# One split instruction per weight granule in place of two, on two engines, in the expert loop of a two-layer trunk

## The reference

```
def swiglu(v, wg, wu, wd):
    return (jax.nn.silu(v @ wg) * (v @ wu)) @ wd

def moe_swiglu(v, router, wg, wu, wd):        # v: 256 x 1024
    ...                                       # combine: 256 x 8, two non-zero per token
    for e in range(N_EXPERTS):                # 8 experts, wg, wu: 1024 x 2816, wd: 2816 x 1024
        y = y + combine[..., e:e + 1] * swiglu(v, wg[e], wu[e], wd[e])
```

## Time and profile before

| | before |
|---|---|
| median of 3 runs | 1849.8 us (1849.54 to 1851.08) |
| profiled execution, own time | 1847.36 us |
| its span, first to last instruction | 1845.6 us |
| mean granted TensorE clock | 0.954 |
| PE busy | 1659.2 us, 90% of the span |
| DVE busy | 1309.2 us, 71% |
| ACT busy | 999.0 us, 54% |
| chain that ended last | PE 85%, DVE 7%, ACT 3% |

### The profile page before, as it was taken

One profiled execution on the slowest core, in us unless ns is written; L12 is line 12 of the kernel. 1 busy time (PEld: TensorE's weight loads), 2 busy tenths in 40 slices (PEclk: granted clock), 3 DMA queues, 4 the chain that ended last, 5 costly groups with the idle time before them and its releaser, 6 DMA issues.

```text
span 1845.6 us, 22715 instructions
## 1 busy us (share of the span) xinstructions
PE 1659.2 (90%) x7728; PEld 1355.5 (73%) x7728; DVE 1309.2 (71%) x1517; ACT 999.0 (54%) x1261; POOL 43.7 (2%) x73
## 2 busy tenths in 40 slices
PE   2997897799986898988769999899999999899976
PEld 2886785688865786777667888788777888788755
DVE  3467687455554466688549898798979898798973
ACT  2454533344443353633337777677777777677752
POOL 2000100000000010010000000000000000000000
PEclk9998999999998899999969999999999999999988
DMA  5442444355653342434439999899989999899950
GB/s 200 155 160 92 137 137 150 118 178 187 199 180 128 109 159 93 137 114 137 151 107 356 341 346 330 306 350 335 352 295 352 346 342 330 302 352 333 354 186 35
DMA packets 292140, 413.94 MB, mean 224 GB/s; under 512 B 15904, under 2 KB 221728, under 8 KB 292000
## 3 DMA queue, kind: packets, MB, share of 16 engines
q1 hardware_dynamic: 286336, 406.41, 65.3%
q10 hardware_dynamic: 5664, 5.81, 1.0%
HBM read 411.11 MB, written 1.05 MB: 223 GB/s over the span
## 4 chain that ended last, share of the span: by engine, by line
PE 85%; DVE 7%; ACT 3%; issue 2%; DMA 1%; POOL 1%; ACTq 0%; DVEq 0%; POOLq 0%
PE ps L1128 25%; PE ps L1130 24%; PE ps L1129 24%; PE ps L1445 2%; PE ps L1331 1%; DVE wlo L704 1%; PE ps L1451 1%; PE ps L1174 1%; ACT whi L442 1%; PE ps L1432 1%; PE ps L1431 1%; DVE arena L721 1%; DMA router<-in_moe_router 1%; ACT arena L472 1%; DVE arena L768 1%
## 5 line engine op out<-in xcount | busy, mean ns | idle before, releaser
L704 DVE TENSOR_TENSOR wlo<-arena,whi 128x1024 fp32r<-128x1024 f32 x774 | 910.6, 1219 | 255.1 <-ACT whi L442 244.0
L442 ACT ACTIVATE whi<-arena 128x1024 fp32r<-128x1024 f32 x774 | 773.8, 1051 | 263.7 <-PE ps L1130 255.1
L1128 PE MATMUL ps<-whi,ahi 128*128 128x512 f32 (+1 forms) x2040 | 829.7, 407 | 40.9 <-issue 16.1
L1130 PE MATMUL ps<-wlo,ahi 128*128 128x512 f32 (+1 forms) x2040 | 804.6, 394 | 0.0
L1129 PE MATMUL ps<-whi,alo 128*128 128x512 f32 (+1 forms) x2040 | 804.0, 394 | 0.0
L1128 PEld LDWEIGHTS ps<-whi,ahi 128*128 128x128 f32 x2040 | 390.0, 191 | 129.0 <-issue 26.1
L1130 PEld LDWEIGHTS ps<-wlo,ahi 128*128 128x128 f32 x2040 | 388.9, 191 | 83.9
L1129 PEld LDWEIGHTS ps<-whi,alo 128*128 128x128 f32 x2040 | 390.3, 191 | 79.6 <-issue 4.3
L704 DVE TENSOR_TENSOR alo<-ps,ahi 128x256 fp32r<-128x256 f32 (+3 forms) x159 | 87.2, 553 | 87.2 <-ACT ahi L442 68.6
L1174 PE MATMUL ps<-ident,arena 128*128 128x128 f32 x128 | 25.1, 377 | 85.5 <-DVE arena L721 80.4
L442 ACT ACTIVATE ahi<-ps 128x512 fp32r<-128x512 f32 (+2 forms) x71 | 43.0, 617 | 105.3 <-PE ps L1404 34.5
(11 more groups left out here) (194 smaller groups left out, 806.6 us busy)
## 6 DMA issues: line engine op xcount, KB each, us to landing
arena<-in_moe_wg SPq DMA_DIRECT2D x176, 512.0 KB, 5.0
arena<-in_moe_wu SPq DMA_DIRECT2D x176, 512.0 KB, 6.5
arena<-in_moe_wd SPq DMA_DIRECT2D x176, 512.0 KB, 6.0
arena<-in_w_in SPq DMA_DIRECT2D x112, 512.0 KB, 4.5
arena<-in_w_branch SPq DMA_DIRECT2D x24, 512.0 KB, 4.2
arena<-in_dense_wg SPq DMA_DIRECT2D x22, 512.0 KB, 3.9
arena<-in_dense_wu SPq DMA_DIRECT2D x22, 512.0 KB, 4.9
arena<-in_dense_wd SPq DMA_DIRECT2D x22, 512.0 KB, 4.0
```

The costliest lines, as they stand in the source:

```text
L442: return nc.scalar.activation(dst, src, ACT.Copy)
L704: return V.tensor_tensor(dst, src, hi.bitcast(f32), ALU.subtract)
L1128: TE.matmul(o, ahi[:, sa], whi[:, sw], start=start, stop=False)
L1130: return TE.matmul(o, ahi[:, sa], wlo[:, sw], start=False, stop=stop)
```

## The change

In the expert loop ACT splits a granule by one copy of 2048 columns, and DVE by one subtraction of 2048 columns, which waits for the whole copy. Each counts its semaphore by two at its end, so that the values that others wait for stay the same. Outside the loop the splits stay in halves.

```
-                                split_hi((M0 + m) % WR, raw((m + WR) % RAW_MOE), 512)
+                                copy(whi[:, (M0 + m) % WR * GRAN:((M0 + m) % WR + 1) * GRAN], raw((m + WR) % RAW_MOE))\
+                                    .then_inc(hi_ready, 2)
...
-                                split_lo((M0 + m) % WR, raw((m + WR) % RAW_MOE), 512,
-                                         lambda i: dve.wait_ge(hi_ready, it * (4 * PER_E) + 2 * (M0 + m + WR) + i + 1))
+                                ring = slice((M0 + m) % WR * GRAN, ((M0 + m) % WR + 1) * GRAN)
+                                dve.wait_ge(hi_ready, it * (4 * PER_E) + 2 * (M0 + m + WR) + 2)
+                                lo_of(wlo[:, ring], raw((m + WR) % RAW_MOE), whi[:, ring]).then_inc(lo_ready, 2)
```

## The result

The changed kernel takes 1865.9 us (median of 4 runs, 1864.55 to 1866.50) beside 1849.7 us: a ratio of 1.0086, with a 95% interval of 1.0068 to 1.0103. It is 16.2 us slower. 1861.7 us was forecast, with a range of 1855 to 1868. Its profiled execution has a span of 1864.0 us, 18.4 more than before; the forecast sum was 11.9.

What follows compares the result with a forecast made beforehand. PE, busy 99.96 of 100 in the loop, was taken to bound the kernel; delayed splits would add 6.5 + 2.6 + 2.0 + 0.8 = 11.9 us to 1849.8, giving 1861.7 us, range 1855 to 1868.

Steps and rivals of the forecast that it cites:

- The sizes of the instructions: Expert loop's splits: ACT's copy of 2048 columns would take 1.93 us, DVE's subtraction of 2048 columns 2.29 us.
- 0.81 us of delay: Every split in the loop: complete 0.81 us later, since DVE can start only after ACT's whole copy.
- ordinary steps: Steps away from the named places: splits stay hidden behind two granules of PE's work, 5.5 us against 5.3; no cost.
- Place A: Slice 10's transposes, 8 times: PE already waits for DVE's silu product behind k = 29's split; 8 x 0.81 = 6.5 us.
- B: Next expert's tokens, 4 times: their low part behind k = 31's split comes late for PE's granule 0; 2.6 us.
- C: Placement of tokens, 8 times: slice 2's low part, behind split and placement on DVE, comes late for down(2); 2.0 us.
- Place D: End of the loop, once: PE waits for DVE's add to h behind the last split; 0.8 us.
- Place E: Start of each pass, 4 times; the forecast had no term for it, 0 us.
- The small products have their own margins: Small DVE products of slices 0 to 9: wanted only after two more granules, so no cost.
- fourth rival: Faster at the three jumps: fewer ACT and DVE instructions to fetch, 7.5 us back; 1846 us if Place A costs 4; chance 2%.
- falling clock at place A: PE's longer waits at Place A lower its clock, eight times 2.7 us, adding 22 us: 1884 us; chance 5%, shared with late DMAs.
- DVE that sets the pace: Whole loop: DVE is the pace, so 264 granules x 0.07 us = 18.5 us come back: 1831 us; chance 1%.

Runs made afterwards that it cites:

- single-step run: The kernel before, with long instructions on both engines in step k = 29 alone; 1853.9 us, ratio 1.0026.
- two one-engine runs: Changed kernel with DVE back in halves that wait for ACT's whole copy, 1865.8 us; kernel before with long subtraction on DVE alone, 1866.5 us.
- interleaved one: Kernel before, splits in halves, with DVE's next wanted small operation between the two halves in k = 29, 30, 31; 1845.6 us, ratio 0.9978.
- table load first: Changed kernel with a one-element copy on ACT at the head of each pass, putting the table load ahead of the wait for PE; 1867.1 us, ratio 1.0104.

## Why the prediction was right, and where it was not

The measured time lies in the range, and the mechanism is the one that was forecast: the two halves let DVE work one half behind ACT, the long instructions put them one behind the other, and PE pays at the places where a small operation stands behind a split in DVE's list and is wanted at once. The single-step run and the two one-engine runs show it. Point by point:

- **The sizes of the instructions** and the 0.81 us of delay (0.87) were right, and so was that ordinary steps cost nothing: the distance of the transposes moves by at most 0.04 us there.
- **Place A**, 6.5 us: 6.9. Here a wait that existed already passed the delay on one to one, 0.86 of 0.87 us, and it was the safest term of the sum.
- **Places B and C** were there, but mis-sized: 2.6 and 2.0 us were 3.7 and 5.0. The step that failed is first the restart of PE. I allowed 0.06 us from DVE's end to the matmul and up to 0.2 for a weight load, and for C I took 0.25 in all. At C, DVE ends the low part at 1091.11 (1090.70 + 0.41), and PE:

```profile
1090.64 0.39 PE L1132 MATMUL ps<-wlo,ahi 128*128 128x512 f32 x1
1091.35 0.49 PE L1130 MATMUL ps<-whi,ahi 128*128 128x512 f32 x1 [0.32 <-DVE alo L705]
1091.68 0.39 PE L1131 MATMUL ps<-whi,alo 128*128 128x512 f32 x1
```

  The matmul was due at 1090.87 and starts 0.24 us after its data are ready, and the next one comes 0.33 instead of 0.23 us later. Of a delay of 0.24 us the program pays 0.62. At B, in the same way, the data are 0.60 us late (DVE ends at 1062.51, the matmul was due at 1061.91 and starts at 1062.75) and the program pays 0.92. Second, the data came 0.12 us later than I had worked out at both places (0.48 us at B, 0.12 at C). For the transposes at A no restart shows, since they started 0.06 us after DVE in both kernels.
- **Place D**, 0.8 us: PE's wait went from 2.49 to 3.34 us, 0.85; the 1.0 of the table is all the growth behind the last transpose.
- **Place E** was missed: 6.8 us where the sum had nothing. "The small products have their own margins" was worked out in mid expert, not at the head of a pass, where two table loads stand in ACT's list; and one of them had moved behind a wait. The order of the changed kernel showed that before any run.
- **The jumps** gave back 5.7 us, the direction of the fourth rival, which held 7.5 us possible. Of it 3.3 are the shorter pauses (14.4 to 11.1), the rest is a shorter stay at 1.2 GHz behind them (0.83 before and 0.91 after over 20 us at each jump). Its reason, fewer instructions for ACT and DVE to fetch, isn't borne out.

So two errors of opposite sign, 6.8 too little and 5.7 too much, nearly cancel, which is luck, and what is left over is B and C: of some 24 us that came and went, the sum had 12. The rivals of a falling clock at place A and of a DVE that sets the pace didn't come about: the clock read 1.00 in the stretches without a jump. The Trainium skill's sentence, in "Perfetto Trace Analysis", section Optimizing Scalar/DVE Operations, that breaking up an instruction may let work be completed sooner on an engine that isn't saturated, is what these runs show, with 0.87 us per split; the saving of 0.07 us on each engine per granule bought nothing on PE.

**What stays open.** PE's pause at a jump is 3.0 to 3.8 us in eight kernels and up to 5.6 in the kernel before, in the one with a single long step (4.52, 3.72, 5.16) and in the interleaved one (4.36, 4.41, 2.72). The traces show what goes with it, though no run was made for it. The view of the DMA queues has one of kind "instruction", q8, that moves 16 KB about every 26 us; I take it for PE's own, since PE alone gets through so many instructions. Over the whole program, the kernel before, then the changed one; then 1 us in the first pause of the kernel before, and the whole first pause (3.8 us) of the changed one:

```profile
q8 instruction: 71, 1.16, 0.3%
q8 instruction: 68, 1.11, 0.2%
...
q8 instruction: 2, 0.03, 22.6%
q8 instruction: 1, 0.02, 1.9%
```

The three kernels with pauses above 4 us have 71 of these transfers, the eight others 68: one more at each jump. In each of the eight pauses above 4 us, the two profiles of the kernel before counted, two of them overlap and the later one takes 2.0 to 2.3 us; in the 28 shorter pauses the last one stands by itself and takes 1.1 to 1.2. Either way PE starts 1.7 to 2.3 us after the last has ended. So PE's pause reads as the wait for its own instructions, and the long ones as two fetches in each other's way. Why three kernels fetch once more at a jump isn't known: PE's program is the same, and neither ACT's nor DVE's length alone decides it.

## What to carry to other kernels

Two engines that work on one buffer one behind the other should hand it over in pieces, unless everything behind it in the second engine's list has more room than one piece takes; here 23 of 33 steps had the room, and the 10 ahead of the places were kept in halves (k = 29 alone, made long, cost 6.9 us). That mix, with the wanted small operation between two halves, made the best kernel, though most of what it gained on the kernel before lies at the jumps. Look for the places by asking of each wait that already exists what stands ahead of its releaser, and work out the heads and ends of loops apart from the steady state. A new pause of PE ahead of a matmul cost its delay and about 0.35 us more for the restart here (0.92 us for 0.60, 0.62 for 0.24), one that was there already only grew by the delay; and the clock can take back what a repair gains, as in the run with the table load first.

## What the runs showed of the hardware that was not expected

- An activation table load can carry the wait of the instruction behind it, and then its 1.28 us come after the wait and not ahead of it.
- Behind a jump the time at 1.2 GHz varies though the pauses are alike. Over 20 us around a jump the granted clock was 0.91 after pauses of 3.60 to 3.76 us (changed kernel), 0.83 after 3.66 to 3.70 (table load first) and 1.00, no fall at all, after 3.66 us (first jump, long subtraction on DVE alone). It varies between two executions of one kernel too: 0.76 and 0.88 over the same 14 us.
- At a jump back PE stood still until 1.7 to 2.3 us after a transfer of 16 KB in an instruction queue had ended, and two such transfers that overlapped made pauses of 4.4 to 5.6 us out of 2.7 to 3.8.
- ACT's copy has 0.84 ns per column (1.913 us at 2048, 1.051 at 1024) and DVE's subtraction 1.05 (2.292 and 1.221), and neither slows the other while both run: instructions that ran wholly beside a busy other engine and those that ran mostly alone differ by under 0.5%.
